# Loading and stacking head 0's queries and keys later, behind the last chunks of the start stage

## The reference

```
h = rmsnorm(x, norm_w) @ w_in
(qa, ka, va, ga, qb, kb, vb, gb, qc, kc, vc, ks, vs, kw, vw, gl, gc) = split(h, columns)
# A: 4 heads, two maps per head with 32 columns each, both causal with a distance penalty
probs = lambda q, k: softmax(where(dist >= 0, q @ k.T * 32 ** -0.5 - slope * dist, NEG))
oa = (probs(q1, k1) - lam * probs(q2, k2)) @ va
# C: keys and values compressed in blocks of 32 tokens by a small network
kcmp = silu(blocks(kc) @ wk1) @ wk2 ; vcmp = silu(blocks(vc) @ wv1) @ wv2
y = x + concatenate([ya, yb, yc]) @ w_out
```

## Time and profile before

| what | us |
|---|---|
| median of three runs (851.9, 852.1, 855.04) | 852.1 |
| the profiled execution, one of these runs | 855.04 |
| its span in the profile | 853.2 |
| PE busy in the span | 770.1 |
| DVE busy | 569.4 |
| ACT busy | 424.3 |
| POOL busy | 125.7 |

### The profile page before, as it was taken

One profiled execution on the slowest core, in us unless ns is written; L12 is line 12 of the kernel. 1 busy time (PEld: TensorE's weight loads), 2 busy tenths in 40 slices (PEclk: granted clock), 3 DMA queues, 4 the chain that ended last, 5 costly groups with the idle time before them and its releaser, 6 DMA issues. The chain is left out here.

```text
span 853.2 us, 16051 instructions
## 1 busy us (share of the span) xinstructions
PE 770.1 (90%) x6224; PEld 658.4 (77%) x6224; DVE 569.4 (67%) x1333; ACT 424.3 (50%) x964; POOL 125.7 (15%) x69
## 2 busy tenths in 40 slices
PE   4899999898898989877989998889998989889996
PEld 4799988676677767666868887778887888778885
DVE  6962111046889998838746987999998889823332
ACT  5631111132656565636743331868888988721221
POOL 0000000020000000002115422333031342132220
PEclk9999999999999999869999998999999999979998
DMA  7211124334242422144135331400001111034421
GB/s 298 105 66 59 38 99 131 103 99 135 62 116 67 133 71 66 50 111 130 40 92 159 100 88 52 112 2 3 2 2 51 51 51 51 3 122 148 147 99 50
DMA packets 31644, 71.82 MB, mean 84 GB/s; under 512 B 5072, under 2 KB 13648, under 8 KB 30544
## 3 DMA queue, kind: packets, MB, share of 16 engines
q1 hardware_dynamic: 31568, 70.78, 27.2%
HBM read 54.52 MB, written 16.25 MB: 83 GB/s over the span
## 5 line engine op out<-in xcount | busy, mean ns | idle before, releaser
L1636 ACT ACTIVATE n_probs<-n_probs,n_negated_max 128x640 f32<-128x640 f32 (+7 forms) x128 | 94.2, 736 | 36.2 <-DVE n_negated_max L1705 36.1
L1714 DVE SCALAR_TENSOR_TENSOR n_probsT_low<-n_turned,n_probsT_high 128x512 f16<-128x512 f32 (+3 forms) x192 | 94.3, 519 | 14.8 <-ACT n_probsT_high L1646 12.7
L708 PE MATMUL n_turned<-identity,n_probs 128*128 128x128 f32 x528 | 82.0, 279 | 12.0 <-ACT n_probs L1636 8.4
L1646 ACT ACTIVATE n_probsT_high<-n_turned 128x512 f16<-128x512 f32 (+3 forms) x192 | 80.1, 452 | 2.4 <-PE n_turned L708 1.6
L1817 PE MATMUL n_scores<-w_and_keys_high,stacks 128*128 128x256 f32 (+2 forms) x192 | 75.6, 394 | 5.3 <-DVE n_negated_max L1705 4.0
L708 PEld LDWEIGHTS n_turned<-identity,n_probs 128*128 128x128 f32 x528 | 59.7, 142 | 25.5 <-ACT n_probs L1636 23.9
L1818 PE MATMUL n_scores<-w_and_keys_low,stacks 128*128 128x256 f32 (+2 forms) x192 | 62.2, 334 | 0.0
L622 PE MATMUL nat<-stacks,xT_high 128*128 128x256 f32 (+1 forms) x192 | 56.0, 292 | 2.5 <-issue 2.2
L623 PE MATMUL nat<-stacks,xT_high 128*128 128x256 f32 (+1 forms) x192 | 55.2, 287 | 0.0
L624 PE MATMUL nat<-stacks,xT_low 128*128 128x256 f32 (+1 forms) x192 | 55.1, 287 | 0.0
L2013 PE MATMUL o_acc<-stacks,o_yT_high 128*128 128x512 f32 x128 | 51.8, 405 | 2.7 <-POOL o_yT_low L1986 2.7
(11 more groups left out here) (258 smaller groups left out, 2184.9 us busy)
## 6 DMA issues: line engine op xcount, KB each, us to landing
w_raw<-in_w_feat SPq DMA_DIRECT2D x23, 512.0 KB, 4.1
features<-staged SPq DMA_DIRECT2D x30, 256.0 KB, 2.6
a_raw<-features SPq DMA_DIRECT2D x36, 128.0 KB, 2.7
s_raw<-features SPq DMA_DIRECT2D x18, 256.0 KB, 4.2
branches_b_c<-in_x SPq DMA_DIRECT2D x8, 512.0 KB, 6.2
silu_gates<-staged SPq DMA_DIRECT2D x16, 256.0 KB, 2.0
gatesT<-silu_gates SPq DMA_DIRECT2D x8, 512.0 KB, 5.2
keys_and_w_out_raw<-in_w_out SPq DMA_DIRECT2D x4, 1024.0 KB, 4.9
```

The costliest lines, as they stand in the source:

```text
L708: mm = nc.tensor.transpose(dst[:, j, :], src[:, c:c + P], ident[:, :])
L1636: nc.scalar.activation(pr[:, n % PS, 0:w], pr[:, n % PS, 0:w], ACT.Exp, scale=-1.0, bias=nmax[:, hb % 4, qt:qt + 1], accum_out=sums[:, hb ...
L1646: nc.scalar.activation(pth[:, g % GS, 0:k, :], tp[g % TS][:, 0:k, :], ACT.Copy, scale=PSCALE).then_inc(t_high, 1)
L1714: nc.vector.scalar_tensor_tensor(out=ptl[:, g % GS, 0:k, :], in0=tp[g % TS][:, 0:k, :], scalar=PSCALE, in1=pth[:, g % GS, 0:k, :], op0=ALU ...
```

## The change

In the loop over chunks the preparation of head 0 is moved back. On SP the 12 transfers stood in pass 5 ahead of the two stores of chunk 5; now they stand behind them, ahead of the weight load of pass 6. On ACT the four high parts stood at the head of pass 6; now they stand behind the split of chunk 7 and the copies of compressed keys and values, ahead of the copy of the left half of chunk 6. On DVE the two low parts stood at the head of pass 6; now they stand behind the split and `keys_and_values`, ahead of the copy of the right half. POOL's list is as it was. No instruction is added, taken away or resized, and no semaphore value changes.

```
--- before.py
+++ after.py
@@ SP, loop over chunks
                 load_chunk(c + 2)
-                if c == WITH_HIDDEN:
-                    sp.wait_ge(hidden, 2)
-                    for h in range(2):
-                        sp.wait_ge(f_out[h], 16 * WITH_HIDDEN)
-                    for j in range(4):
-                        src = feat_dram[(QA, KA)[j % 2][0], A_QK * (j // 2):A_QK * (j // 2 + 1), :]
-                        for band in range(3):
-                            sp.dma_start(a_raw[A_QK * band:A_QK * (band + 1), j, :], src).then_inc(a_raw_in, 16)
                 store(c)
...
+                if c == WITH_HIDDEN:
+                    (the same eight lines)
@@ ACT, loop over chunks
-                if c == WITH_SECOND:
-                    for j in range(4):
-                        a_stack(j)
                 split_chunk(c + 1)
...
                             nc.scalar.copy(vc3[part, g, 0, :], vp[g][part, 0:HD]).then_inc(first, 1)
+                    for j in range(4):
+                        a_stack(j)
                 evacuate(c)
@@ DVE, loop over chunks
-                if c == WITH_SECOND:
-                    (the two low parts of the queries)
                 split_chunk(c + 1)
                 if c == WITH_HIDDEN:
                     hidden_units()
                 if c == WITH_SECOND:
                     keys_and_values()
+                    (the two low parts of the queries)
                 evacuate(c)
```

More of the change, by code:

```diff
@@ L352, in _ @@
                             sp.dma_start(cc[HD:P, group, 0:S - 1], src[:, 1:S]).then_inc(cc_in, 16)
+                if c == WITH_HIDDEN:
+                    sp.wait_ge(hidden, 2)
+                    for h in range(2):
+                        sp.wait_ge(f_out[h], 16 * WITH_HIDDEN)
+                    for j in range(4):
+                        src = feat_dram[(QA, KA)[j % 2][0], A_QK * (j // 2):A_QK * (j // 2 + 1), :]
+                        for band in range(3):
+                            sp.dma_start(a_raw[A_QK * band:A_QK * (band + 1), j, :], src).then_inc(a_raw_in, 16)
         @block.scalar
@@ L571, in _ @@
             for c in range(LAST):
+                split_chunk(c + 1)
+                if c == WITH_HIDDEN:
+                    hidden_units()
                 if c == WITH_SECOND:
+                    keys_and_values()
                     for j in range(0, 4, 2):
@@ L578, in _ @@
                                                        op0=ALU.mult, op1=ALU.subtract)
-                split_chunk(c + 1)
-                if c == WITH_HIDDEN:
-                    hidden_units()
-                if c == WITH_SECOND:
-                    keys_and_values()
                 evacuate(c)
```

## The result

The changed kernel takes 858.4 us (median of 5 runs) against 851.9 in the same series: the ratio is 1.0066, 95% interval 1.0039 to 1.0093. It is slower, by 5.6 to 7.3 us according to the series and to whether the ratio or the medians are taken; the two intervals reach from 3.3 to 8.3. The profiled execution has a span of 855.7 us and a time of 857.5.

The account below looks back on a forecast made before the run. PE, busy 90% of the span, was taken to bound the kernel. A block start 5.8 us later plus 2.2 us of lower clock gave 8.0 over the median 852.1: 860.1 us, range 856.0 to 863.5.

Parts of the forecast that it names:

- PE sets the block end before, the stack work costs nothing there: Block end before the change: PE ends at 196.8, others follow within a microsecond; stack work, over by 192.1, costs nothing.
- The transfers begin at 186.2 and ACT at 195.2: SP queue: 12 transfers issued 186.2 to 192.6, stacks whole 2.6 us later, so ACT's four copies start at 195.2.
- DVE and POOL take turns, POOL is last, at 203.3: Low parts of the stacks: DVE and POOL alternate from 196.3, and POOL arrives last at the block end, 203.3.
- Block start 5.8 us later: PE's start of the next block: about 204.1 instead of 198.31, 5.8 us later, bounds 4.9 to 6.5.
- The clock costs 2.2 us (1.7 to 2.8): After 7.3 us of PE idleness the next block starts at the lower clock for 3.4 to 5.7 us, losing 2.2.
- the clock costs nothing: Rival for the next block: clock back in time or its loss falls into ACT and DVE waits; 857.9 us, chance 0.15.
- Faster, by what later low stretches return: Rival: full speed in later low stretches, chiefly 357.3 to 377.8, returns up to 10.3 us; 849.8 or 847.6, chance 0.03.
- the low stretch at 156 to 159: PE's lower clock from 155.96 to 159.34, 3.4 us, after a 2.21 us gap; half of a low stretch is lost.

Follow-up runs that it names:

- e1: Kernel before with only ACT's four stack copies and DVE's two low parts moved late, SP's 12 transfers early as before: 852.7 us, ratio 1.0003.
- e4: Kernel before, nothing moved, three POOL operations with unused results added to wait for PE's last matmul of the stage: 858.7 us, ratio 1.0086.
- e8: Kernel before with PE's left half of the features of chunk 5 put ahead of the compression: 854.7 us, ratio 1.0036.
- e2: Kernel before with only SP's 12 transfers moved behind both stores of chunk 5, copies early as before: 864.7 us, ratio 1.0145.
- e9: Kernel before with 24 matmuls of unused result added on PE behind its last of the stage, nothing else late: ratio 1.0074.

## Why the prediction was right, and where its steps were not

The forecast was 860.1 us, 8.0 over the median, range 856.0 to 863.5; measured were 858.4 and, against 851.9, 6.5 over it (5.6 by the ratio, 6.6 by that of the second series).

- *PE sets the block end before, the stack work costs nothing there.* Right. e1 moves the copies with no change to the time; e4 needs nothing but a late arrival.
- *The transfers begin at 186.2 and ACT at 195.2.* They began at 185.95 and ACT at 194.91. Two terms behind it were off and cancelled: the issue took 5.5 us (the lower bound named, and not the 6.4 taken), and the stacks were whole 3.5 us after the last issue ended, where the rows gave 2.6.
- *DVE and POOL take turns, POOL is last, at 203.3.* Right: 202.7. The low part of DVE that is alone took 1.21, the second 2.62 for 2.7 expected. The copy out of PSUM was not held up beside POOL, as the prediction took it and as no row of before could show. The Trainium skill ("GPSIMD Engine Reference", Key points) names DVE instructions with two SBUF inputs or in a 2-port mode as those that contend with GpSimd; this copy has no SBUF input, and the trace agrees with its 0.69 us.
- *Block start 5.8 us later.* Measured 5.05, inside the bounds of 4.9 to 6.5. The rest of the difference is the step from the last arrival to PE's start, taken as 0.8 from DVE's end before; it is 0.34 behind POOL's.
- *The clock costs 2.2 us (1.7 to 2.8).* By the second scores it cost 2.9, a little beyond the upper bound, since the level came back only 6.3 us after the restart. That it is passed on whole to the end is the step that **failed**: three kernels without this low stretch are no faster. The rival "the clock costs nothing" gave 857.9, nearer to the 858.4 measured than the forecast of 860.1 and with the better mechanism for that half. That the forecast's range holds the measurement is owed to the block start and to the width of the range; in the place of the 2.2 us of the clock stand microseconds that no step of the prediction names, and that is luck. But the ratios of the late kernels stand for 5.6 to 9.3 us, with block starts 4.2 to 5.4 us later behind PE's last matmul of the stage; in most of them 1 to 2 us, as far as the intervals allow to say, come on top of the late start, with a warm restart as with a cold one. What it is stays open.
- *Faster, by what later low stretches return.* Not seen in any late kernel; the long one is still there in the changed kernel, 20.4 us from 363 on. What the profile of one execution gives back or takes in them is several microseconds and says little of the median: the changed kernel's profiled span is only 2.5 us above that of before, with the block start 4.7 later.
- The prediction called the low stretch at 156 to 159 a loss of half its length in passing, and e8's expectation counted on 1.7 us from it. That was wrong too, see below: e8's PE ended its stage 2.5 us earlier, about the 2.2 us of the gap, and not 3.9.

## What to carry to other kernels

At a place where all engines meet, ask of every engine when it arrives; work that is hidden is hidden only as long as its end lies before the last arrival, and moving the transfer it waits for behind a store that itself waits for the current tile moves all of it. An instruction in a transfer queue takes on every wait ahead of it: here one place in SP's list, ahead of or behind one store, was 4 to 5 us. And of a term that shows in the trace 15 us after the edit, test whether it is still there at the end before it goes into the sum.

## What the runs showed of the hardware

**The lower clock did not slow the compression matmuls.** In the stretch of 157 to 158 us, PE at the lower level in the kernel before:

```profile
157.00:158.00 1.00, 1.00 (x5) 0.50 0.01 4
```

and in e1, which had no low stretch there:

```profile
157.00:158.00 1.00, 1.00 (x5) 1.00 0.06 4
```

Both began these 64 matmuls of 128x189 float32 at 153.4 to 153.5 and the first matmul behind them at 173.7: 20.25 us, with 3.4 us of low clock and without. (Their weight loads did take longer: 2.81 us busy for ten of them in 156 to 159 us, against 1.93 in e1.) The 128x512 matmuls of the rounded type go from 0.23 to 0.43 us apart. Why the two kinds differ is not shown. So what a low stretch costs depends on which matmuls it meets.

**A small DVE operation can wait for the whole of a POOL operation.** Four casts of 63x64 between two tiles in SBUF, beside POOL's low parts in e1 (duration in ns: minimum, median, maximum):

```profile
L528 DVE CAST cmp_values<-c_value_rest x4: 188/192/2351, 188.7 to 189.4; 63x64 bf16<-63x64 f32 x4
```

Three took their usual 0.19 us. The last started at 189.4, just after POOL's first low part (189.27 to 191.67), and took 2.35. In e2 the subtraction of 1.23 us took 3.27 in the same way; a copy from PSUM kept its 0.69. Two engines that are idle for much of the time can so be late together.

**Where PE arrives last, the next block starts after 0.3 us** (e9), and 0.34 us after POOL in the changed kernel. The 1.53 us of before are mostly the half copy on DVE (to 197.51, 0.7 us behind PE) and the last store behind it (to 197.86); the start follows 0.45 us later.
